# Even attention: where the two halves of a unit pair's value products stand in TensorE's queue

## What is computed

```python
s = jnp.einsum('bqhmd,bkhmd->bhmqk', q, k).astype(jnp.float32) * (A_QK ** -0.5)
p = jax.nn.softmax(s, axis=-1)
a = p[:, :, 0] - lam * p[:, :, 1]
return jnp.einsum('bhqk,bkhd->bqhd', a, v.astype(jnp.float32))
```

## Time and profile before

| what | value |
|---|---|
| median of 3 runs | 2229.4 us (2227.24 to 2231.35) |
| the profiled execution, its time | 2231.54 us |
| its span | 2229.8 us |
| mean granted TensorE clock | 0.981 of full speed |

### The profile page before, as it was taken

How to read it: one execution, slowest core, us unless ns; L and a number is a source line. 1 busy time by engine, 2 the same in 40 slices (tenths; PEclk the granted TensorE clock), 3 DMA queues, 4 the chain that set the end, 5 groups by cost and what they waited for, 6 DMA issues and landing times.

```text
span 2229.8 us, 28649 instructions
## 1 busy us (share of the span) xinstructions
PE 2166.6 (97%) x12030; PEld 1781.1 (80%) x12030; DVE 1362.0 (61%) x1795; ACT 559.0 (25%) x1105; POOL 48.1 (2%) x31
## 2 busy tenths in 40 slices
PE   8999998899999999999999999999999999999998
PEld 5788885668788668887888888888888888888887
DVE  6134449894651474785787753654888437977633
ACT  4010007752220462373311110221100003111101
POOL 0000000000010020300000000000000000000000
PEclk9899997999899999999999999999999999999999
DMA  9133322312131021202222223322221332222322
GB/s 368 72 113 114 114 81 55 86 47 95 57 120 62 21 74 57 95 2 95 86 104 95 95 78 104 102 94 95 76 95 62 99 104 93 97 90 98 106 95 76
DMA packets 34240, 204.54 MB, mean 92 GB/s; under 512 B 4800, under 2 KB 5056, under 8 KB 14656
## 3 DMA queue, kind: packets, MB, share of 16 engines
q1 hardware_dynamic: 32736, 197.99, 25.6%
q10 hardware_dynamic: 1376, 4.72, 0.6%
HBM read 191.16 MB, written 2.10 MB: 87 GB/s over the span
## 4 chain that ended last, share of the span: by engine, by line
PE 86%; DVE 9%; ACT 2%; issue 2%; DMA 1%; DVEq 0%; SPq 0%; ACTq 0%
PE ps L437 23%; PE ps L439 22%; PE ps L438 22%; PE ps L538 3%; PE ps L539 3%; PE ps L540 3%; DVE stat L2252 2%; PE ps L695 2%; PE ps L1348 1%; PE ps L589 1%; PE ps L1040 1%; PE ps L572 1%; PE ps L807 1%; DVE prob L2279 1%; PE ps L582 0%
## 5 line engine op out<-in xcount | busy, mean ns | idle before, releaser
L1956 DVE CAST whi<-raw 128x2048 fp32r<-128x2048 f32 (+2 forms) x148 | 172.2, 1164 | 430.8 <-DMA raw<-in_ffn_out 106.6
L437 PE MATMUL ps<-h2hi,whi 128*128 128x512 f32 (+1 forms) x1084 | 417.4, 385 | 2.8 <-DVE h2lo L2078 2.4
L439 PE MATMUL ps<-h2hi,wlo 128*128 128x512 f32 (+1 forms) x1084 | 413.2, 381 | 0.0
L438 PE MATMUL ps<-h2lo,whi 128*128 128x512 f32 (+1 forms) x1084 | 413.2, 381 | 0.0
L1959 DVE TENSOR_TENSOR wlo<-raw,whi 128x2048 fp32r<-128x2048 f32 (+2 forms) x148 | 320.2, 2163 | 5.1
L437 PE MATMUL ps<-h1hi,whi 128*128 128x512 f32 (+1 forms) x768 | 269.9, 351 | 2.0 <-ACT y L1389 1.2
L438 PE MATMUL ps<-h1lo,whi 128*128 128x512 f32 (+1 forms) x768 | 267.0, 348 | 0.0
L439 PE MATMUL ps<-h1hi,wlo 128*128 128x512 f32 (+1 forms) x768 | 266.8, 347 | 0.0
L437 PEld LDWEIGHTS ps<-h2hi,whi 128*128 128x128 f32 x1084 | 204.3, 188 | 43.8 <-DVE h2lo L2078 2.5
L439 PEld LDWEIGHTS ps<-h2hi,wlo 128*128 128x128 f32 x1084 | 204.4, 189 | 39.0
L438 PEld LDWEIGHTS ps<-h2lo,whi 128*128 128x128 f32 x1084 | 204.5, 189 | 38.2
(11 more groups left out here) (330 smaller groups left out, 3338.3 us busy)
## 6 DMA issues: line engine op xcount, KB each, us to landing
raw<-in_ffn_in SPq DMA_DIRECT2D x44, 1024.0 KB, 4.9
raw<-in_even SPq DMA_DIRECT2D x16, 1024.0 KB, 7.2
mod_w<-in_mod SPq DMA_DIRECT2D x6, 2048.0 KB, 19.6
raw<-in_odd SPq DMA_DIRECT2D x12, 1024.0 KB, 4.9
raw<-in_sgu_v SPq DMA_DIRECT2D x12, 1024.0 KB, 4.9
raw<-in_sgu_u SPq DMA_DIRECT2D x12, 1024.0 KB, 4.9
raw<-in_sgu_out SPq DMA_DIRECT2D x16, 768.0 KB, 4.2
raw<-in_ffn_out SPq DMA_DIRECT2D x16, 704.0 KB, 4.0
```

The lines of the kernel that those rows point to most:

```text
L437: pe.matmul(o, r(lhi), r(rhi), start=first, stop=False, **kw)
L438: pe.matmul(o, r(lhi), r(rlo), start=False, stop=False, **kw)
L439: return pe.matmul(o, r(llo), r(rhi), start=False, stop=last, **kw)
L1956: step(dve.tensor_copy(whi[:, slot, 0:width].bitcast(F32R), raw[:, slot, 0:width]))
```

## The change

Half 0 of a pair's value products, which stood in odd units, moves one unit later, in front of half 1 in the even unit. An odd unit then issues no value products, an even unit issues both halves one after the other, behind the late transposes of the unit before. For wide pairs an even unit's block grows from 12 to 24 instructions. Half 0 of pair 22 leaves the loop and goes behind it. No DMA, no buffer and no other engine's queue is edited, and half 0's wait moves with it.

```diff
                 if u:
                     even_transposes(u - 1, range(4, 6), moved[u] - 1)
-                if u >= 3:
-                    even_pv((u - 3) // 2, (u - 3) % 2)
+                if u >= 4 and u % 2 == 0:
+                    even_pv((u - 4) // 2, 0)
+                    even_pv((u - 4) // 2, 1)
                 pe.wait_ge(ea["probs"], u + 1)
                 if t < 4:
                     even_transposes(u, range(4), moved[u])
+            even_pv((last_unit - 2) // 2, 0)
             even_pv((last_unit - 2) // 2, 1)
             even_transposes(last_unit, range(4, 6), moved[last_unit + 1] - 1)
             even_pv(last_unit // 2, 0)
```

## The result

The changed kernel takes 2244.41 us, median of six runs (2238.18 to 2248.80), against 2229.77 for six runs of the kernel before on the same chip: a ratio of 1.0063 [1.0048, 1.0078], slower by 14.6 us. A later measurement of the same kernel, on another chip, gave 1.0038 [1.0022, 1.0054]. The forecast was 2232.9 with a range up to 2236.5, and a difference too small to be measured was held for likeliest; the change costs about two to three times the 0.2% named for that.

A forecast was written before the change was run, and what follows sets the result against it. VectorE was taken to bound wide units; TensorE, ScalarE's copies and exponentials the narrow ones. Exits 0.45 + 0.62 + 0.93 + 1.15 plus 2 x 0.2 made 3.55 us, on 2229.4 giving 2232.9, range 2228.4 to 2236.5.

The forecast's parts named there:

- rival C: All 23 pairs: saved tiling-mode switches free at most 0.145 us each, 6.7 us of TensorE's queue, giving 2222.7; chance 0.08.
- The sum for the queue: Even-attention stage: four exits from wide into narrow units plus two half-clock stretches cost 3.55 us in all.
- The exit of hp = 2: Wide-to-narrow exit of hp = 2: no convolved tile covers unit 34's doubled products, so the maxima of 37 come 0.93 us later.
- Those of hp = 0 and 1: Wide-to-narrow exits of hp = 0 and 1: VectorE gets its scores 0.45 and 0.62 us late.
- Step 1: Exit of hp = 1: ScalarE is free for the early copy of 17 at 397.05, not 396.63, 0.42 us later.
- Step 3: Exit of hp = 1: unit 19 without products returns 0.81 us, but its early transposes come 0.27 late, waiting for probs.
- Wide units at nothing: Among wide units, the added half's 0.66 us is just covered by slack, 0.02 left: cost 0, by a hair.
- the dearer half: Case in which the added half takes 0.81 us: 0.15 more at each of 16 wide pairs, 2.4 us, giving 2235.3.
- 0.2 each: Two half-clock stretches: early transposes behind joined narrow halves wait longer, 0.2 us per stretch, between 0 and 0.4.
- rival A: Behind hp = 2: TensorE's clock falls once more for 6.8 us, costing 1 to 2 us, giving 2234 to 2235.3; chance 0.17.
- Rival B: Copies and exponentials have more slack than counted; only the stage's end costs, 1.15 us, giving 2230.5; chance 0.13.
- Rival D: Narrow pairs, 4 instructions a half: joining changes next to nothing, taking 0.4 us off, giving 2232.5; chance 0.62 together with forecast.

The follow-up runs named there:

- e2: The changed kernel, plus six transposes of the identity (two for narrow pairs) in each odd unit at half 0's old place: 2231.83 us, ratio 1.0012.
- e7: The kernel before, plus sixteen identity transposes in odd unit 11 of each hp but the last, that pair's half 0 one unit later: 2229.01 us, 1.0006.
- e1: The changed kernel, with half 0's products issued once more in the odd units and overwritten later: 2233.46 us, ratio 1.0020.
- e5: The changed kernel, with identity transposes filled in only in odd units 7, 9 and 11 of each hp: 2234.62 us, ratio 1.0023.
- e9: The changed kernel with half 0 of every pair's value products left out altogether, half 1 keeping its place: 2238.02 us, ratio 1.0030.
- e4: The changed kernel with halves joined only where the even unit is narrow and behind the loop, other pairs in the old order: 2239.86 us, 1.0037.
- e8: The kernel before, plus identity transposes between the column sums ahead of the next stage: 2231.82 us, ratio 1.0016.

## Why the prediction was wrong

**The block and the queue: right.** The second half behind the first was put at 0.66 and the block at 1.47 to the early transposes; in the trace the first product stands at 400.19 and the transposes at 401.66, 1.47. No product stands in an odd unit. The switch saved is real, 2 x 0.81 - 1.47 = 0.15 a pair, and yet nothing of it reached the time (rival C). The Trainium skill, "TensorEngine Tiling (Array Packing)", Tiling Modes, says that a change of the tiling mode drains TensorE, and these rows agree with it.

**The sum for the queue: right in size, not in each place.** Four exits and the half-clock stretches came to 3.55. The change's profile lost 3.44 in four steps without dear falls, and some 0.9 more at the stage's end. The exit of hp = 2 can be read cleanly, as it lies wholly at full clock: 0.93 was said, 0.87 is there (8.01 to 8.87). Those of hp = 0 and 1 were put too low: 0.45 and 0.62, and 0.9 each was gone by units 8 and 20, before a fall set in. Two steps of the working for hp = 1 were off. Step 1 has ScalarE free for the copy of 17 at 397.05, though exp1(18), by the paragraph before it, ends at 397.16; it came at 399.18, 2.55 later than the 396.63 of the earlier trace rows, and 2.00 of that is what unit 17 was late already: 0.55, not 0.42. Step 3 has the products taken out of unit 19 return 0.81, so that early T(19) comes 0.27 late. It came 2.79 later than before, less the same 2.00: 0.79 late, at full clock. The row at 404.00, shown above, has it waiting 0.57 for ScalarE's copy of the late transposes ahead of it: the time freed became a wait. ScalarE's copy of 17 in the changed kernel, then TensorE's early T(19) in the kernel before:

```profile
399.18 0.60 ACT L1391 ACTIVATE ept<-ps 128x512 f32<-128x512 f32 x1
```

```profile
401.21 0.65 PE L695 MATMUL ps<-mats,prob 128*128 128x128 f32 x4
```

e2 bears the sum out from another side: its stage is 2.71 - (-1.38) = 4.1 us longer than e7's, both at full clock behind the start, though either holds filling of its own. By units 10, 31, 40 and the end this splits into 1.3, 0.3, 0.8 and 1.7, where the exits had 0.45, 0.62, 0.93 and 1.15: that the sum agrees better than its terms is in part luck.

**Wide units at nothing: near enough.** From unit 28 to unit 31 the shift stayed at 8.01, so the pace of 3.05 us held there; from unit 16 to unit 18 it grew by 0.12, where 0 "by a hair" was said and 0.15 with the dearer half.

**The term that failed: the clock.** The prediction put "0.2 each" on the two half-clock stretches and nothing in the sum on any more of them; one more fall stood apart as rival A, at 1 to 2.4 us, with a chance of 0.17, "behind hp = 2". What came is six stretches in place of two, in four dear steps of 12.7 us, about 1 of it the queue. Three things were wrong in it.

*What makes the clock fall.* In the earlier trace rows there were pauses of 1.75 and 2.06 ahead of the falls and 1.08 where none came, and the prediction took the pause for the cause. The exit of hp = 2 in the changed kernel, at full clock throughout, speaks against this (TensorE's timeline):

```profile
448.76 1.53 PE L839 MATMUL ps<-ept,ev 128*64 128x128 f32 x24
...
452.22 0.50 PE L807 MATMUL ps<-wlo,whi 64*128 64x256 f32 x2 [1.13 <-ACT prob L1586]
...
453.59 1.53 PE L839 MATMUL ps<-ept,ev 128*64 128x128 f32 x24
...
458.09 0.50 PE L807 MATMUL ps<-wlo,whi 64*128 64x256 f32 x2 [1.60 <-ACT prob L1586]
```

Here stand pauses of 1.13 and 1.60, the second about what was worked out (1.4), and no fall; while the fall at 405.50 has, from 393 on, nothing longer ahead of it than the 0.57 at 404.00. For the two falls of the kernel before the pause stays possible. The Trainium skill, "TensorE: Matmul & The Clock Gate", HAM oscillation, speaks of gaps between bursts of matmuls; here the rows do not bear it out as the whole cause. What brings the added falls, by e1, e2, e5 and e9, is odd units without products: fill their place with products or transposes and most of the falls go, leave half 0 out and they come with no block grown. The products that the diff takes out of the odd units had held the clock there; the prediction counted those of unit 19 as 0.81 returned.

*How long it lasts.* 6.8 us were taken, as in the earlier trace rows. The two dearest last 13.7 and 10.2.

*What it costs.* The price, 2.4 at most, came from stretches in which VectorE was busy for 6.53 and 5.82 of 6.80 and so covered most of it; e7 shows those two to be worth 1.3 together. At the exits VectorE waits for TensorE, and there the joined block is dearest: 2.83 - 1.53 = 1.30 more for each, twice behind each other at hp = 1 and at the end. The step with the fall at hp = 1 cost 4.6, beyond the 1.1 that before's own second fall costs there by e7; that at the end cost about 4, its step of 5.0 less the queue. Cover does not explain all of it: the fall at 470.3 lies among wide units, with VectorE busy for 3.10 of 3.40, and its step still cost 1.5.

Rival B (all covered) and C (the switches bring time) fell with the first number. Rival D, that the change does next to nothing at narrow pairs, looked at the narrow pairs' products, and what costs are blocks that stand in narrow units: e4, which moves no others but that behind the loop, has 9.2 us of the stage. What the list of signs called wrong, "if a third stretch at half clock stands behind hp = 2", was the right sign in the wrong place.

Left open: why the falls sit in the same places in the change's two profiles, and what brought those at 385.0, 422.5 and 470.3, which lie among wide units, where e5 leaves such stretches too; whether the head sums have a part in it, as both long falls of the change begin within them (those at 405.00 and at 483.47), though none begins in e2's at 400.10; what the queue alone costs to the tenth, since e1 and e2 hold extra work; and whether some arrangement with the joined blocks can come out ahead. None of the kernels here measurably beat the one before; e7, which is the kernel before with filling, comes closest to equal at 1.0006.

## What to carry to other kernels

Before work is taken out of a thin stretch of TensorE's queue, or moved within it, look at what is left there: the granted clock of the stretches is a term of the sum, and here it outweighed the queue by about three to one. A unit that keeps only a few small matmuls and transposes may be at full clock because of the very work that is to go, and filling the hole with transposes whose result nobody uses is a quick way to tell the two causes apart. Price a fall by who waits for TensorE at that place, not by the falls that the profile happens to show where another engine covers them.

## What was not expected of the hardware

- Half of the products left out makes the kernel slower, 1.0030 [1.0013, 1.0046], with falls of 61.5 us together.
- In the odd units of this stage transposes of the identity hold the clock as well as products do: 1.00 in e2, 0.99 in e1, 0.87 without either. Between the column sums of e8 they did not bring it back.
- The clock fell at 405.50 with TensorE idle for 0.57 us at most from 393 on, stayed up across one of 1.60 (458.09), and stays at 0.50 for 20.5 us with TensorE busy for 19.12 of them (563.0 in the kernel before).
